# Moving three groups of modulation products from the context's attention into the latent's, and fetching two groups earlier

## What is computed

```python
def modulation(cvec, w_mod, b_mod):
    m = jax.nn.silu(cvec) @ w_mod + b_mod
    return jnp.split(m[:, None, :], N_MOD, axis=-1)

for i in range(DEPTH):
    ml = modulation(c, w_mod[i], b_mod[i])
    mc = modulation(c_ctx[None, :], w_mod[i], b_mod[i])
    hl = modulate(rmsnorm(xl, g_pre_mix[i]), ml[0], ml[1])
    hc = modulate(rmsnorm(xc, g_pre_mix[i]), mc[0], mc[1])
    ...
    xl_new = xl + ml[2] * rmsnorm(y_l, g_post_mix[i])
    h2 = modulate(rmsnorm(xl_new, g_pre_mlp[i]), ml[3], ml[4])
    xl_new = xl_new + ml[5] * rmsnorm(sqrelu_mlp(h2, w_mlp_in[i], w_mlp_out[i]), g_post_mlp[i])
    ...
```

## Time and profile before

| | |
|---|---|
| median of three runs | 2936.13 us |
| the profiled execution, its own time | 2935.57 us |
| its span (first to last instruction) | 2934.2 us |
| TensorE matmuls busy | 2836.1 us, 97% of the span |
| VectorE, ScalarE, GpSimd busy | 1356.9, 1125.4, 1277.9 us |
| moved by DMA | 291.67 MB, mean 99 GB/s |

### The profile page before, as it was taken

How to read it: one execution, slowest core, us unless ns; L and a number is a source line. 1 busy time by engine, 2 the same in 40 slices (tenths; PEclk the granted TensorE clock), 3 DMA queues, 4 the chain that set the end, 5 groups by cost and what they waited for, 6 DMA issues and landing times.

```text
span 2934.2 us, 40890 instructions
## 1 busy us (share of the span) xinstructions
PE 2836.1 (97%) x16278; PEld 2341.0 (80%) x16278; DVE 1356.9 (46%) x2527; ACT 1125.4 (38%) x1917; POOL 1277.9 (44%) x828
## 2 busy tenths in 40 slices
PE   7789999999999999989999899999999999999999
PEld 6577778888888786778888787888878878888887
DVE  5448643241211576632211457776542368667432
ACT  4353554553332444543332344332433344323332
POOL 4253247874444442344444353343534433435343
PEclk9899999999999999999999999999999999999999
DMA  7834114653233324033333222111223221212222
GB/s 260 307 106 152 39 49 151 181 160 101 94 94 129 113 82 144 1 108 94 96 93 102 71 97 69 58 58 58 87 72 94 77 89 49 68 58 72 85 73 87
DMA packets 81981, 291.67 MB, mean 99 GB/s; under 512 B 9216, under 2 KB 9600, under 8 KB 81408
## 3 DMA queue, kind: packets, MB, share of 16 engines
q1 hardware_dynamic: 81792, 289.06, 30.6%
HBM read 286.93 MB, written 2.10 MB: 99 GB/s over the span
## 4 chain that ended last, share of the span: by engine, by line
PE 84%; DVE 10%; ACT 2%; issue 2%; POOL 1%; DMA 1%; SPq 0%; POOLq 0%; ACTq 0%; DVEq 0%
PE ps L625 65%; PE ps L598 5%; DVE ps L2263 4%; PE ps L769 3%; PE ps L790 2%; PE ps L958 1%; PE ps L653 1%; PE ps L1021 1%; PE ps L1032 1%; PE ps L894 1%; PE ps L1199 1%; DVE t L2555 1%; DVE t L2593 1%; POOL t L2895 1%; PE ps L907 0%
## 5 line engine op out<-in xcount | busy, mean ns | idle before, releaser
L625 PE MATMUL ps<-t,t 128*128 128x512 f32 (+3 forms) x9936 | 2210.7, 380 | 20.9 <-DVE t L2027 7.4
L625 PEld LDWEIGHTS ps<-t,t 128*128 128x128 f32 x9936 | 1778.5, 189 | 366.5 <-issue 33.1
L2895 POOL TENSOR_TENSOR t<-t,t 128x1024 fp32r<-128x1024 f32 (+3 forms) x444 | 1041.0, 2348 | 1105.4 <-ACT t L1335 1064.9
L1335 ACT ACTIVATE t<-t 128x1024 fp32r<-128x1024 f32 (+3 forms) x444 | 457.9, 1035 | 855.1 <-PE ps L625 806.0
L598 PE MATMUL ps<-t,t 128*128 128x128 f32 (+2 forms) x1662 | 237.5, 279 | 33.9 <-DVE t L2078 12.2
L598 PEld LDWEIGHTS ps<-t,t 128*128 128x128 f32 (+2 forms) x1662 | 190.4, 141 | 80.9 <-ACT t L1448 16.1
L2366 DVE TENSOR_TENSOR ps<-ps,t 128x512 f32<-128x512 f32 (+1 forms) x96 | 57.2, 606 | 344.1 <-ACT t L1641 344.1
L2379 DVE TENSOR_TENSOR t<-ps,t 128x512 f32<-128x512 f32 x60 | 40.9, 692 | 217.6 <-PE ps L625 217.5
L2263 DVE SCALAR_TENSOR_TENSOR ps<-t,t,ps 128x512 f32<-128x512 f32 (+1 forms) x174 | 116.1, 667 | 6.4 <-ACT ps L1556 0.6
L2915 POOL TENSOR_TENSOR t<-t,t 128x4 f32<-128x4 f32 (+2 forms) x93 | 85.6, 921 | 75.3 <-DVE t L2036 39.3
L769 PE MATMUL ps<-t,t 96*128 96x384 f32 (+1 forms) x320 | 105.6, 453 | 4.8 <-DVE t L2126 2.4
(11 more groups left out here) (264 smaller groups left out, 2398.8 us busy)
## 6 DMA issues: line engine op xcount, KB each, us to landing
t<-in_wbig SPq DMA_DIRECT2D x412, 512.0 KB, 3.5
t<-in_wmod SPq DMA_DIRECT2D x96, 512.0 KB, 6.5
t<-in_wbig SPq DMA_DIRECT2D x16, 416.0 KB, 3.2
t<-in_wbig SPq DMA_DIRECT2D x14, 256.0 KB, 2.7
t<-in_wbig SPq DMA_DIRECT2D x8, 332.0 KB, 3.0
t<-in_wbig SPq DMA_DIRECT2D x6, 384.0 KB, 3.1
t<-in_x SPq DMA_DIRECT2D x1, 2048.0 KB, 8.2
out<-t SPq DMA_DIRECT2D x8, 256.0 KB, 2.1
```

The costliest lines, as they stand in the source:

```text
L625: m = p.matmul(out, lhs, rhs, start=kk == 0 and n == 0, stop=kk == tiles - 1 and n == 2)
L1335: a.activation(c.hi(w), c.raw(w), ACT.Copy).then_inc(w_hi.h, w_hi.up(("cut", w)))
L2895: g.tensor_tensor(c.lo(w), c.raw(w), c.hi(w).bitcast(F32), ALU.subtract).then_inc(w_lo.h, w_lo.up(("cut", w)))
```

## The change

Groups (0,9), (0,10) and (0,11) leave the context's heads. The four that stay are woven in at 0.25, after the steps 3, 7, 11 and 15. (0,9) takes the place of (1,0) in l0's mix, (0,10) that of (1,1) behind it, and l0's heads get six groups, (0,11) and (1,0) to (1,4), at the steps 3, 8, 13, 18, 23 and 28. In l1's heads the three groups stand at the steps 4, 9 and 14. Of the buffers, set 4 is used by (0,6) and (0,10) only; from (0,11) on all groups but (1,5) and (1,11) use set 0. The quarters of (0,4) are issued among the last weights that zt frees, those of (0,5) among sc's, while before they came among sb's, and behind (0,7).

```diff
@@ fetches, free
-                if u == (0, 4):
-                    return at[("w", self.of[("sc", "c0")][q])]
+                if u in ((0, 4), (0, 5)):
+                    return at[("w", self.of[("zt" if u[1] == 4 else "sc", "c0")][q])]
...
-                least = {(0, 6): ("sb", "c0"), (0, 5): ("wkv", "c0"), (1, 1): ("sb", "l0"), (1, 5): ("w1", "ml0", 3, 0),
-                         (1, 6): ("w2", "ml0", 3, 1), (1, 7): ("sb", "l1"), (1, 11): ("wo", "l1", 0)}.get(u)
+                least = {(0, 6): ("sb", "c0"), (0, 10): ("sb", "l0"), (1, 5): ("w1", "ml0", 3, 0),
+                         (1, 6): ("w2", "ml0", 3, 1), (1, 11): ("wo", "l1", 0)}.get(u)
@@ mod_set
-        if n < 13:
-            return (0, 1, 2, 3, 0, 2, 4, 0, 2, 4, 0, 4, 0)[n]
-        return {17: 3, 23: 1}.get(n, 4 if n % 2 else 0)
+        if n < 9:
+            return (0, 1, 2, 3, 0, 2, 4, 0, 2)[n]
+        return {10: 4, 17: 3, 23: 1}.get(n, 0)
@@ pe_program; the programs of ScalarE, VectorE and GpSimd change alike
-    rest = onward(weave(heads("c0"), mods(0, 5, 12, [6, 7]), 0.45, -1.0), 2 * NH + 2)
+    rest = onward(weave(heads("c0"), mods(0, 5, 9, [6, 7]), 0.25, -1.0), 2 * NH + 2)
...
-    run(beside(weave(mix("l0"), g, 0.5), mods(1, 0, 1, [2, 6]), (56,)))
-    run(mods(1, 1, 2, [2, 3]))
-    rest = onward(beside(heads("l0"), mods(1, 2, 5, [6, 7]), (4, 5, 12)), 4 * NH + 2)
+    run(beside(weave(mix("l0"), g, 0.5), mods(0, 9, 10, [2, 6]), (56,)))
+    run(mods(0, 10, 11, [2, 3]))
+    groups = chain(mods(0, 11, 12, [6, 7]), mods(1, 0, 5, [6, 7]))
+    rest = onward(beside(heads("l0"), groups, (3, 8, 13, 18, 23, 28)), 4 * NH + 2)
...
-    rest = onward(beside(heads("l1"), mods(1, 7, 10, [6, 7]), (4, 5, 12)), 4 * NH + 2)
+    rest = onward(beside(heads("l1"), mods(1, 7, 10, [6, 7]), (4, 9, 14)), 4 * NH + 2)
@@ sp_program, fetch_mod
-        if i == 1 and g in (1, 3, 7, 9):
-            S.wait_ge(gemm, ("end", ("sb", "l1" if g > 6 else "l0")))
+        if (i, g) == (0, 10):
+            S.wait_ge(gemm, ("end", ("sb", "l0")))
```

More of the change, by code:

```diff
@@ L1937, in act_program @@
     run(steps)
-    rest = onward(weave(heads("c0"), mods(0, 5, 12), 0.45, -1.0), 2 * NH + 2)
+    rest = onward(weave(heads("c0"), mods(0, 5, 9), 0.25, -1.0), 2 * NH + 2)
     row_of("c0")
@@ L1942, in act_program @@
     run(beside(weave(project("c0"), both(rest, g, 4), 1.0), only(g, 3), (11, 14, 15)))
-    run(beside(weave(mix("l0"), g, 0.5), mods(1, 0, 1), (56,)))
-    run(mods(1, 1, 2))
-    rest = onward(beside(heads("l0"), mods(1, 2, 5), (4, 5, 12)), 4 * NH + 2)
+    run(beside(weave(mix("l0"), g, 0.5), mods(0, 9, 10), (56,)))
+    run(mods(0, 10, 11))
+    groups = chain(mods(0, 11, 12), mods(1, 0, 5))
+    rest = onward(beside(heads("l0"), groups, (3, 8, 13, 18, 23, 28)), 4 * NH + 2)
     row_of("l0")
@@ L1961, in act_program @@
     run(mods(1, 6, 7))
-    rest = onward(beside(heads("l1"), mods(1, 7, 10), (4, 5, 12)), 4 * NH + 2)
+    rest = onward(beside(heads("l1"), mods(1, 7, 10), (4, 9, 14)), 4 * NH + 2)
     row_of("l1")
@@ L2844, in dve_program @@
     run(beside(weave(project("c0"), both(rest, g, 4), 1.0), only(g, 3), (11, 14, 15)))
-    run(beside(weave(mix("l0"), chain(g, residual("c0", 1)), 0.6), mods(1, 0, 1), (56,)))
+    run(beside(weave(mix("l0"), chain(g, residual("c0", 1)), 0.6), mods(0, 9, 10), (56,)))
     for i in range(L):
@@ L3236, in pool_program @@
     run(beside(weave(project("c0"), both(rest, steps, 4), 1.0), only(steps, 3), (11, 14, 15)))
-    run(beside(weave(mix("l0"), then(steps, residual, "c0"), 0.6), mods(1, 0, 1), (56,)))
-    run(mods(1, 1, 2))
-    rest = onward(beside(heads("l0"), mods(1, 2, 5), (4, 5, 12)), 4 * NH + 2)
+    run(beside(weave(mix("l0"), then(steps, residual, "c0"), 0.6), mods(0, 9, 10), (56,)))
+    run(mods(0, 10, 11))
+    groups = chain(mods(0, 11, 12), mods(1, 0, 5))
+    rest = onward(beside(heads("l0"), groups, (3, 8, 13, 18, 23, 28)), 4 * NH + 2)
     next(rest)
```

## The result

The changed kernel takes 2939.92 us, the median of 15 executions (2935.2 to 2943.78), against 2935.3 for the kernel before, also of 15 (2929.7 to 2937.35). The ratio is 1.0017, with a 95% interval of [1.0009, 1.0025]: slower by 2.6 to 7.3 us. The forecast was 2933.0, from a sum of -2.8 us, with a range of 2926 to 2940, so the time lies at the upper edge of the range and on the other side of no change. The profiled execution took 2939.92 too, with a span of 2938.5.

What follows compares the result with a forecast made beforehand. TensorE was taken as the bound, with gaps in the context's heads and almost none in the latent's. Terms of -15.7 there and +12.9 here gave -2.8 us, forecast 2933.0 us, range 2926 to 2940.

Steps and rivals of the forecast that it cites:

- the extra in the context's heads: Context's heads: time beyond the groups' bare work, said to go with the change, in parts of 3.7, 1.1, 1.7 and 3.7 us.
- -3.7 for (0,5): Context's heads: group (0,5) takes 6.62 us, needs 2.0 plus 0.9 for copies; early quarters save 3.7 us.
- -1.1 for the two steps behind it: Context's heads, 102.63 to 107.20: two steps at half clock take 4.57 us against 3.4 at full clock, saving 1.1.
- -1.7 for (0,6): Context's heads: group (0,6) takes 3.73 us against 2.0 at full clock, saving 1.7.
- -3.7 for (0,8): Context's heads, behind step 8's put: the 2.15 us bank wait and slow work of (0,8) and following logits go, saving 3.7.
- The latent's part: Latent's heads, l0 and l1: three more groups +6.0, bank waits +4.7 and +1.3, clock +0.9, together +12.9 us.
- The bank waits don't cost: Rival, latent's heads: bank waits are made good where TensorE would have waited later; sum -9.7 us, 2925.9; chance 0.21.
- The context's heads stay at half clock: Rival, context's heads: less dense stage, so the clock still falls and 6.5 us aren't won; +3.7, 2939.3; chance 0.11.
- Half clock in the latent's heads: Rival, latent's heads: bank waits each bring a stretch of half clock; +9.9 us, 2945.5; chance 0.06.
- One set isn't enough: Rival, shortest gap, (1,6) to (1,7): with the longest landing the fetch comes 4.9 us late; 2937.7; chance 0.05.
- The early quarters delay the weights: Rival, context's mix: the additional early quarters delay the context's weights; +1.6 us, 2934.4; chance 0.05.
- The costs set at nothing: DMAs and queues: early quarters, the later issue of X and later group fetches stay hidden, costing 0 us.

Runs made afterwards that it cites:

- e1: The kernel before, unchanged, profiled a second time: 2931.22 us.
- e12: e4 with group (0,4) on bank 6 instead of bank 2: 2927.95 us, ratio 0.9977.
- e3: The kernel before with only the quarters of group (0,5) fetched early, all groups left in place: 2929.91 us, ratio 0.9984.
- e8: e3 with the groups of the context's heads at steps 2, 4, 6, 9, 11, 13, 15, none right behind the put: 2926.0 us, ratio 0.9980.
- e7: The changed kernel with the early fetch undone, the moved groups kept: 2941.26 us, ratio 1.0024.
- e2: The changed kernel, unchanged, profiled a second time: 2940.8 us.
- e11: The kernel before, unchanged, profiled a fourth time: 2936.50 us.
- e4: The changed kernel with groups at steps 5, 9, 13, 17, 21, 28 in l0's heads and 4, 9, 13 in l1's: 2933.29 us, ratio 0.9988.
- e10: The kernel before, unchanged, profiled a third time: 2936.77 us.
- e6: The changed kernel with seven eighths of the matmuls of groups (1,0), (1,2) and (1,4) left out: 2935.07 us, ratio 1.0005.
- e9: e8 with group (0,4) on bank 6 instead of bank 2: 2921.93 us, ratio 0.9955.
- e13: e9 again, the same kernel, run beside e12: 2924.48 us, ratio 0.9965.

## Why the prediction was wrong

**The step that failed** is the extra in the context's heads, in the prediction's words: "The clock explains the lengths", and then -3.7 for (0,5), -1.1 for the two steps behind it, -1.7 for (0,6) and -3.7 for (0,8). These 10.2 us were read as belonging to the places, so that they would go with them; 6.5 of them were the clock, and from (0,4) to l0's mix the change gave 9.8 us, not 15.7. In executions without half clock the stage takes 55.97 us before (e1) and 48.03 with the groups moved (e12): 7.9, and it splits into runs of its own:

- the quarters of (0,5): -1.3 (e1 to e3), where -3.7 stood; in the first trace the four waits were 2.55 together (the first of them in the earlier trace rows), some 1.3 more than this
- the two steps and (0,6): nothing, where -2.8 stood
- (0,8) behind the put: -1.85 (e3 to e8), where -3.7 stood
- three groups less: -4.8 (e8 to e12, 52.80 to 48.03). The forecast was -6.0 + 0.5, so 1.2 and not 0.5 is uncovered: the timeline of the changed kernel in the first section shows waits of 0.92 and 1.18 for a new head's copies, open where the groups stand at odd steps.

This is the price at full clock. On average over 11 executions the early fetch alone gave 4.7 us in the kernel before (e3), so some clock was to be won there; undone in the changed kernel it cost 2.1 by the ratios, 1.3 by the medians (e7). (A slip besides: the bound "-16.5 if nothing is uncovered" should be -16.2, the sum without its +0.5.)

The profiles with half clock say the same by another way. Over the four profiles of before the heads took 60.75 us on average, over the two of after 49.4; but from the start of (0,4) to the group in l0's mix, (1,0) before and (0,9) after, the averages are 185.8 and 175.9, 9.8 less, since part of the half clock was now ahead of the heads and part behind them, from 149 on in e2. From 74 to 460 us the profiles have 17.1 us of half clock on average before and 13.6 after, behind 460 us 31.4 and 35.3, and the mean clock of all executions is 0.9908 before and 0.9905 after. So half clock changed its places, and there wasn't less of it in the whole; whether what came behind 460 us has to do with the change isn't shown. I had taken the first trace's 17 us of half clock in this stage as what there is to be won, and had seen that the same trace has a wait of 3.38 us at 78.64 that brought none. Half clock came with it in e1, in e11 and in both profiles of after, and that one sentence of the prediction ("by none") should have made the clock a term with a range rather than part of the sum.

**The latent's part** was right in kind, place and nearly in size. Forecast: +6.0 for the groups, +4.7 for the banks in l0, +1.3 in l1, +0.9 for the clock, +12.9. Measured in l0: +12.9 in the first profile, +11.3 in e2 (no half clock), so 10.7 without the clock was 0.6 too small; in l1 +1.85 (119.42 to 121.27), with a wait of 0.31 behind the others. On average 12.1 + 1.85.

**The balance** by the averages of four and two profiles: -9.8 up to (0,9), +12.1 in l0's heads, +1.85 in l1's, and +1.3 behind them, where the change touches nothing, and where the fifteen profiles scatter from 1686.8 to 1690.8 us. The scatter goes with the clock: the same stretch has 17.1 to 29.7 us of half clock, 24.6 on average in the four of before and 28.5 in the two of after, and the two figures have a correlation of 0.89, with 0.28 us of time for each us of half clock, which makes 1.1 of the 1.3. Together with -0.1 for the stages between, +5.3, which is the difference of the mean spans (2933.7 and 2939.0); the medians differ by 4.6.

**The rivals.** "The bank waits don't cost" is refuted by e4. "The context's heads stay at half clock", with 2939.3, came nearest in time, in part by luck, and its reason is half right: the clock's 6.5 us were not won, though in the heads themselves the half clock shrank to 3.4 us and the rest came back elsewhere. What was said against it, that "no fall came behind waits as short as these", doesn't hold: in both profiles of after the clock fell inside these heads behind waits of 1.18 us (at 128) and 0.92 (at 102). "Half clock in the latent's heads" was seen once, 3.4 us in one of two profiles. "One set isn't enough": nothing waits for in_wmod there. The Trainium skill, in "Trainium Kernel Development and Optimization", Best Practices, asks for double buffering; by that rule as it stands the nine fetches in set 0 would have been in the open, and the trace disagrees, with 0 us of waits for them, since four to five steps of other work stand between one group and the next. "The early quarters delay the weights": group (0,4) starts at 80.1 us on average before and at 80.0 after, so no.

**The costs set at nothing** held: no wait for in_x, none for in_wmod, no later weights.

## What to carry to other kernels

A stretch of half clock in one profile is not a property of the code it lies over: profile the same kernel several times, and price a step from executions in which it ran at full clock. A stage in which TensorE has gaps is the cheap place for side work, since there a group hides waits that would otherwise be seen (3.95 us came back when 4.6 were cut, against all 4.6 in the dense stage; three whole groups gave back 4.9 us there and cost 7.4 in the other), so emptying it is worth less than the work's own length. And before moving work, look at which bank it waits for: the early fetch, one group a step past the `put` and another bank for one group brought 10 to 13 us together (ratios 0.9965 and 0.9955), where the move of three groups costs 2.9.

## What the runs showed that I had not expected

- Which wait is followed by a fall varies between executions of the same kernel. The wait of 3.4 us ahead of (0,4) was followed by one in six of the first ten profiles; the wait of 2.15 us ahead of (0,8) was in the first trace of before and in e10 and e11, and was not in e1. The Trainium skill says of this, in "TensorE: Matmul & The Clock Gate", The HAM clock gate, that the chip's observation of TensorE runs freely of the kernel's start, so that the place where the clock rises at a kernel's start varies from run to run. The four profiles of before show as much for the falls inside a kernel: the first behind 74 us is at 97, 79, 98 and 80 us.
- A short wait can be followed by a fall too. In e2, e4, e6 and e7 the clock fell at 102, 102, 105 and 99 us, less than a microsecond behind a wait of 0.92 us; in e11 it fell at 97, behind one of 0.52. Nor does a long wait always bring one (e3).
- With the long waits taken away there was little half clock from 74 to 460 us: 0, 0 and 3.4 us in the profiles of e9, e13 and e12, against 6.8 to 20.5 in those of the two kernels. But e3's profile had none either, with both long waits in it, and behind 460 us the three have 17.1, 34.1 and 30.7 us, against 29.4 to 36.5. Over all executions the mean clock rose from 0.9908 to 0.9936 (e9), 0.9926 (e13) and 0.9923 (e12), at 1.6 us for each 0.001; e8, with the wait ahead of (0,4) still there, has 0.9926. That the waits bring the falls is the natural reading, and these runs don't show it.
